# A two-layer diffusion block on one core: the context's hidden values loaded later and in pairs, its FFN output product begun from weight units still in the ring, and another order of the engines beside the first pair of FFN columns

## What is computed

```
for i in range(2):                      # layer 0: window attention || gated linear attention; layer 1: 2-D neighbourhood
    hl = rms_norm(xl, g) * (1 + sc1) + sh1      ;  hc = the same of the context xc
    yl, yc = mixer(hl, hc)
    xl = xl + gt1 * rms_norm(yl)
    xl = xl + gt2 * rms_norm(swiglu(rms_norm(xl) * (1 + sc2) + sh2))
    if i == 0:                          # the context is carried through layer 0 only
        xc = xc + cgt1 * rms_norm(yc)
        xc = xc + cgt2 * rms_norm(swiglu(rms_norm(xc) * (1 + csc2) + csh2))
swiglu(h) = (silu(g) * u) @ w_out,  [g, u] = h @ w_in,   2816 hidden columns
```

## Time and profile before

| | |
|---|---|
| time, median of 3 runs | 1626.89 us (1626.4 to 1628.17) |
| the profiled execution's own time | 1628.51 us |
| its span in the profile | 1626.7 us |
| PE busy | 1581.5 us, 97% of the span |
| DVE, ACT, POOL busy | 64%, 45%, 21% |
| granted clock, mean of the span | 0.995 |
| HBM | 187.97 MB read, 12.88 MB written |

### The profile page before, as it was taken

How to read it: one execution, slowest core, us unless ns; L and a number is a source line. 1 busy time by engine, 2 the same in 40 slices (tenths; PEclk the granted TensorE clock), 3 DMA queues, 4 the chain that set the end, 5 groups by cost and what they waited for, 6 DMA issues and landing times.

```text
span 1626.7 us, 27464 instructions
## 1 busy us (share of the span) xinstructions
PE 1581.5 (97%) x10334; PEld 1384.1 (85%) x10334; DVE 1042.4 (64%) x1710; ACT 738.1 (45%) x1401; POOL 333.7 (21%) x277
## 2 busy tenths in 40 slices
PE   6999999999899999998999999999999999999998
PEld 4878887778899999997887788888888899889986
DVE  5955567718988878867787533017872788258843
ACT  4342226737544444433336442237873645235632
POOL 2311233034000000000002044233433410420042
PEclk9999999999999999999999999999999999999999
DMA  9843211023154344337893539324012233323332
GB/s 356 276 130 82 50 27 53 2 78 91 50 169 128 114 141 142 121 139 247 320 321 131 168 114 243 86 78 130 16 53 77 73 97 109 125 80 106 108 113 76
DMA packets 176371, 204.21 MB, mean 126 GB/s; under 512 B 16664, under 2 KB 138864, under 8 KB 175856
## 3 DMA queue, kind: packets, MB, share of 16 engines
q1 hardware_dynamic: 162232, 156.62, 31.0%
q10 hardware_dynamic: 14008, 45.83, 8.7%
HBM read 187.97 MB, written 12.88 MB: 123 GB/s over the span
## 4 chain that ended last, share of the span: by engine, by line
PE 86%; DVE 5%; ACT 3%; issue 2%; DMA 1%; POOL 1%; SPq 0%; DVEq 0%; ACTq 0%; POOLq 0%
PE ps L2789 26%; PE ps L3347 18%; PE ps L2742 13%; PE ps L2966 11%; PE ps L3159 3%; PE ps L3102 3%; PE ps L3065 3%; PE ps L3022 2%; PE ps L2898 1%; PE ps L3043 1%; PE ps L2859 1%; PE ps L2771 1%; DMA mod_early<-in_w_mod 1%; DVE prob L2060 1%; ACT junk L1251 1%
## 5 line engine op out<-in xcount | busy, mean ns | idle before, releaser
L676 POOL TENSOR_TENSOR w_lo<-w_raw,w_hi 128x1024 fp32r<-128x1024 f32 (+2 forms) x88 | 219.9, 2501 | 642.2 <-ACT w_hi L1264 642.0
L1264 ACT ACTIVATE w_hi<-w_raw 128x1024 fp32r<-128x1024 f32 (+2 forms) x202 | 204.3, 1013 | 212.5 <-PE ps L2789 152.5
L676 DVE TENSOR_TENSOR w_lo<-w_raw,w_hi 128x1024 fp32r<-128x1024 f32 (+1 forms) x111 | 126.7, 1144 | 91.5 <-ACT w_hi L1264 91.3
L2742 PE MATMUL ps<-h_hi,w_hi 128*128 128x512 f32 (+1 forms) x480 | 142.8, 354 | 1.3 <-DVE h_lo L1866 1.1
L3347 PE MATMUL ps<-hc_hi,h_hi 128*128 128x384 f32 x420 | 141.0, 336 | 2.9 <-ACT x_u L1311 2.3
L3347 PE MATMUL ps<-hc_hi,h_lo 128*128 128x384 f32 x420 | 140.3, 334 | 0.0
L3347 PE MATMUL ps<-hc_lo,h_hi 128*128 128x384 f32 x420 | 140.3, 334 | 0.0
L2742 PE MATMUL ps<-h_hi,w_lo 128*128 128x512 f32 (+1 forms) x480 | 140.3, 349 | 0.0
L2742 PE MATMUL ps<-h_lo,w_hi 128*128 128x512 f32 (+1 forms) x480 | 139.5, 348 | 0.0
L2789 PE MATMUL ps<-w_hi,h_hi 128*128 128x512 f32 x408 | 128.1, 395 | 5.3 <-DVE w_lo L676 4.1
L2789 PE MATMUL ps<-w_lo,h_hi 128*128 128x512 f32 x408 | 126.7, 392 | 0.0
(11 more groups left out here) (404 smaller groups left out, 3864.4 us busy)
## 6 DMA issues: line engine op xcount, KB each, us to landing
w_raw<-in_w_ffn_in SPq DMA_DIRECT2D x88, 512.0 KB, 3.9
w_raw<-in_w_ffn_out SPq DMA_DIRECT2D x66, 512.0 KB, 3.9
mod_raw<-in_w_mod ACTq DMA_DIRECT2D x40, 512.0 KB, 6.1
mod_early<-in_w_mod SPq DMA_DIRECT2D x30, 512.0 KB, 10.1
w_raw<-in_na_w_in SPq DMA_DIRECT2D x29, 512.0 KB, 3.7
gate_b<-in_w_mod ACTq DMA_DIRECT2D x18, 512.0 KB, 4.6
hid_far<-full SPq DMA_DIRECT2D x22, 384.0 KB, 2.3
xs<-hid_far SPq DMA_DIRECT2D x22, 256.0 KB, 6.1
```

The lines of the kernel that those rows point to most:

```text
L676: eng.tensor_tensor(w_lo[:, ring(u), cols], w_raw[:, u % RAW, cols], w_hi[:, ring(u), cols].bitcast(F32), ALU.subtract).then_inc(low_ready ...
L1264: act.activation(w_hi[:, ring(u), cols], w_raw[:, u % RAW, cols], ACT.Copy).then_inc(w_hi_done, 1)
L2742: mm = pe.matmul(o[0], sta(x, o), mov(y, o), start=first and n == 0, stop=last and n == 2)
```

## The change

It does five things.

1. **`fo0C` keeps three units.** Its list of new units is cut from 22 to 19; the product begins with units 19, 20 and 21 of `fo0L`, which are in the ring, and takes k = 19, 20, 21 first. Its three early `feed`s among the norms become one (DVE) or none (ACT); PE waits once for all of `hidc_lo`.
2. **The context's hidden values later.** `hidc_turn(k)` says which context parts are handled in iteration k of `fo0L`: none for k under 5, then two in each of 5 to 9, then part k itself. All are split within `fo0L`.
3. **Another order beside pairs 0 and 1** on DVE and ACT: `combine_first` is cut into `first_half`, `first_sums` and `first_made`, which stand at three places; `part_copy(1)` and `part_sum(1)` stand ahead of the last split parts of `hc`; pair 1's jobs `s4` and `a22` are split earlier; sums and scales of the context's norm are interleaved otherwise.
4. **The last unit of `out0L`** gets its low part from DVE instead of POOL.
5. **A Silu of one column** (`warm`) right after the attention, so that ACT's table load stands there.

```diff
-    rows("fo0C", a["w_ffn_out"][0], range(FT))
+    rows("fo0C", a["w_ffn_out"][0], range(FT - KEPT))
...
+    by_dve[sp("out0L") + KT - 1] = True
...
-            for n, name in enumerate(("out0C", "v1C")):
+            for n, name in enumerate(("out0C", "fo0C", "v1C")):
                 if sp(name) <= u < sp(name) + KEPT:
                     eng.wait_ge(w_again, n * KEPT + u - sp(name) + 1)
...
+        def hidc_turn(k):
+            return (2 * k - 10, 2 * k - 9) if 5 <= k < 10 else (k,) if 10 <= k else ()
...
-                if sp("fo0L") + 3 <= u < sp("fo0C") + 3:
-                    hidc_load(u - sp("fo0L") - 3)
+                if sp("fo0L") + 6 <= u < sp("fo0C") + 1:
+                    for k in hidc_turn(u - sp("fo0L") - 1):
+                        hidc_load(k)
...
+            def part_copy(j):
+                act.wait_ge(s_used, NT + job(j, "s1") + 1)
+                act.wait_ge(f_11, NT + j)
+                act.activation(part_p, fast_ps(fast_banks(j)[2]), ACT.Copy).then_inc(fp_copied, 1)
...
                 for k in range(FT):
                     high_jobs(HID_JOB + k)
-                    if k >= 2:
-                        hidc_high(k - 2)
+                    for x in hidc_turn(k):
+                        hidc_high(x)
                     feed(sp("fo0L") + k)
...
             attention(0, 1, last_projection)
+            act.activation(warm[:], one_col[:], ACT.Silu)
...
             for p in range(PARTS):
                 hc_high(6, p)
             high_jobs(job(1, "s3"))
+            high_jobs(job(1, "a22"))
             for p in range(PARTS):
                 hc_high(3, p)
+            part_copy(1)
             for p in range(PARTS):
                 hc_high(5, p)
             high_jobs(job(1, "s2"))
-            act.wait_ge(fp_2, NT + 3)
-            act.activation(sum_11, fast_ps(fast_banks(0)[0]), ACT.Silu).then_inc(f_silu1, 1)
...
             attention(0, last_projection, rotate_add)
+            feed(sp("out0L") + KT - 1)
...
-            def combine_first():
+            def first_half():
...
+            hc_sum(1, 0)
+            hc_sum(2, 0)
             gated("out0C", 0, gb_need["out0C"])
...
             joined("out0C", 1, LT + 1)
-            hc_low(dve, 4, 0)
             pre_scale("ffn0C", 0, C_TILES)
...
             low_jobs(job(1, "s3"))
+            first_half()
             weight_sum(dve, 1, "s2")
             weight_sum(dve, 1, "s4")
             for p in range(PARTS):
                 hc_sum(4, p)
+            first_sums()
+            low_jobs(job(1, "s4"))
             for p in range(PARTS):
                 hc_low(dve, 3, p)
+            low_jobs(job(1, "a22"))
+            part_sum(1)
             for p in range(PARTS):
                 hc_low(dve, 5, p)
             low_jobs(job(1, "s2"))
...
-            tm_product("fo0C", FT, hidc_act, C_TILES, two_halves("fo0C"), before=claim_tile("fo0C"),
+            pe.wait_ge(hidc_lo_done, NT + FT)
+            tm_product("fo0C", FT - KEPT, hidc_act, C_TILES, two_halves("fo0C"), before=claim_tile("fo0C"), kept="fo0L",
                        after=lambda k: out_hooks[k]() if k in out_hooks else None)
```

More of the change, by code:

```diff
@@ L267, in build @@
     by_dve = [False] * n_units
-    for name, n, step in (("fo0L", FT, 1), ("fo0C", FT, 1), ("v1C", KT - KEPT, 1)):
+    for name, n, step in (("fo0L", FT, 1), ("fo0C", FT - KEPT, 1), ("v1C", KT - KEPT, 1)):
         for u in range(sp(name) + step - 1, sp(name) + n, step):
@@ L1308, in fast_in @@
                         break
[L1309 to L1312, removed]
+                    if j > 1:
+                        part_copy(j)
+                    if 1 < j < FT - 1:
                         high_jobs(job(j + 1, "s3"))
@@ L1693, in _ @@
             pre_square("ffn0C", 1, C_TILES, (post_x, POST["out0C"] + 2))
+            hc_high(4, 0)
             hc_high(2, 0)
[L1695 to L1698, removed]
+            pre_high("ffn0C", 0, C_TILES, whole=False)
+            act.wait_ge(fp_2, NT + 3)
+            act.activation(sum_11, fast_ps(fast_banks(0)[0]), ACT.Silu).then_inc(f_silu1, 1)
+            hc_high(4, 1)
+            hc_high(2, 1)
+            pre_high("ffn0C", 1, C_TILES, whole=False)
+            hc_high(4, 2)
+            hc_high(2, 2)
             for p in range(PARTS):
@@ L1731, in _ @@
             for k in range(FT):
-                feed(sp("fo0C") + k + RING)
+                feed(sp("fo0C") + k)
                 if k in hooks:
@@ L2468, in combine_first, with part_sum, sum_first @@
                 dve.tensor_tensor(second, second, columns3(sum_12[:]), ALU.mult).then_inc(hid_made, 1)
+            def part_sum(j):
+                dve.wait_ge(s_used, NT + job(j, "s3") + 1)
+                dve.wait_ge(fp_copied, NT + 2 * j + 1)
+                dve.wait_ge(f_22, NT + j)
+                dve.tensor_tensor(sum_t, fast_ps(fast_banks(j)[3]), part_p, ALU.add).then_inc(f_t, 1)
+            def sum_first(j):
+                dve.wait_ge(w_used, ring_no[sp("fi0") + 2 * j] + 1)
+                dve.wait_ge(fp_copied, NT + 2 * j + 2)
+                dve.tensor_tensor(sum_11, fast_ps(fast_banks(j)[0]), part_p, ALU.add).then_inc(f_11, 1)
             def gated(name, i, need):
@@ L2537, in _ @@
                     break
[L2538 removed]
+                if j == 1:
+                    sum_first(1)
                 if j + 1 < FT:
@@ L2548, in _ @@
                     weight_sum(dve, j + 1, "s4")
-                dve.wait_ge(w_used, ring_no[sp("fi0") + 2 * j] + 1)
-                dve.wait_ge(fp_copied, NT + 2 * j + 2)
-                dve.tensor_tensor(sum_11, fast_ps(a_), part_p, ALU.add).then_inc(f_11, 1)
+                if j > 1:
+                    sum_first(j)
                 low_jobs(job(j + 1, "s2") if j + 1 < FT else HID_JOB + 2)
@@ L2556, in _ @@
                 low_jobs(HID_JOB + k)
-                if k >= 2:
-                    hidc_low(k - 2)
+                for x in hidc_turn(k):
+                    hidc_low(x)
                 feed(sp("fo0L") + k)
                 add_rows(("fo0L", k))
-            for k in (FT - 2, FT - 1):
-                hidc_low(k)
             mix1 = range(NT)
             post_norm("fo0L", 0, 0, FT)
-            feed(sp("fo0C"))
             post_norm("fo0L", 1, 1, FT)
@@ L2568, in _ @@
             post_norm("fo0L", 2, 2, FT)
-            feed(sp("fo0C") + 1)
+            post_norm("fo0L", 3, 3, FT)
+            feed(sp("fo0C"))
             pre_scale("mix1", 1, mix1)
-            post_norm("fo0L", 3, 3, FT)
-            feed(sp("fo0C") + 2)
             hooks = {2: lambda: modulation(7), 3: lambda: (pre_modulate("mix1", 0, mix1), pre_scale("mix1", 2, mix1)),
@@ L2580, in _ @@
             for k in range(FT):
-                if k + RING < FT:
-                    feed(sp("fo0C") + k + RING)
+                if k < FT - KEPT:
+                    feed(sp("fo0C") + k)
                 if k in hooks:
@@ L2765, in again @@
                 def again(n, i, t, last):
-                    k = KT - KEPT + n
+                    k = (FT if kept == "fo0L" else KT) - KEPT + n
                     s = sp(kept) + k
```

52 lines of the change are left out of this document (26 added, 26 removed).

## The result

The changed kernel takes 1620.76 us, median of 20 executions, beside 1628.95 us for the kernel before: a ratio of 0.9949, 95% interval 0.9941 to 0.9958, or 8.2 us (6.8 to 9.6). The forecast was a ratio of 0.9942 and 1617.5 us. It is faster by more than the 0.2% that can be told from no change. But that the sum came out so near is in part luck: the gains are some 3 us larger than forecast, and the change costs 4 us or more in a way that the prediction does not name, by the addresses of tiles that TensorE reads. The two nearly cancel.

A forecast was written before the change was run, and what follows sets the result against it. PE bounds the kernel, working 1581.5 of 1626.7 us. Terms -0.9 - 2.5 - 3.5 - 2.5 = -9.4 us take the profiled 1628.51 to 1619.1, or 1617.5 from the median 1626.89; range 1612.0 to 1623.5.

The forecast's parts named there:

- What is at stake, 18.6 us: Eight PE waits where the change works, 14.1 us, plus lower clock behind two of them, 2.8 and 1.7 us.
- The last unit, -0.9: `out0L`'s tail: with the low part on DVE, PE's wait of 0.93 goes, -0.9 us.
- The first pairs, -2.5: Start of `fi0`: waits of 1.23, 2.31, 0.54 shrink or go, 2.53 for `hc` 4 stays, new 1.3 at pair 2.
- The start of `fo0L`, -3.5: The 4.07 wait at unit 2 and its 2.8 of clock go, 6.9 us; 3.5 kept after later limits.
- the second limit: `fo0L` soon after 786 us: DMA engines full, 1.9 us spare at unit 17, loads forward by only 1 to 2 us.
- The ring of pairs: `fo0L` iterations 5 to 9: two buffers, each pair loaded after the last is split; unit 10 ready at 795.3, 2.3 us lost.
- L = 5: Assumed time in us from issue to landing of a pair of context parts in `fo0L`.
- The start of `fo0C`, -2.5: With three units already in the ring, PE's waits of 1.12 and 1.40 for low parts go, -2.5 us.
- A: Rival: `fo0L` keeps its whole 6.9 us and pair 2's new wait doesn't come; 14.1 in all, 1612.8 us; chance 0.20.
- B: Rival: pairs land at 6.2 us, `fo0L` loses 1.4 instead of winning 3.5; 4.5 in all, 1622.4 us; chance 0.17.
- D: Rival: pairs land at 8.5 us, unit 10 of `fo0L` 12.9 later; 7.0 slower, 1633.9 us; chance 0.08.
- C: Rival: the first pairs give nothing, DVE's full list just moves the waits; 6.9 in all, 1620.0 us; chance 0.09.

The follow-up runs named there:

- x1_kept: The kernel before with only the three kept units of `fo0C` (with its feeds, norms and waits); 1626.25 us, 0.9982.
- x4_lastunit: The kernel before with only the low part of `out0L`'s last unit moved to DVE; 1627.97 us in one execution.
- y3_turn: The changed kernel with the context's second-tile turn ahead of pair 1's product 2 on PE, and `hc` 4's low parts ahead of `hc` 2's on DVE; 1619.87 us, 0.9954.
- z3_nowarm: The changed kernel without the warm Silu and without its tile; 1617.16 us, 0.9920.
- z1_wide: The changed kernel with the warm Silu's tile 16 columns wide instead of one, the Silu still writing one column; 1618.62 us, 0.9932.
- z4_best: The changed kernel with the 16-column warm tile, four buffers for the context's hidden values, and pair 2's low part made ahead; 1617.21 us, 0.9926.
- y1_nofirst: The changed kernel with the order beside pairs 0 and 1 as before, the other four edits kept; 1623.72 us, 0.9973.
- z2_pad: The kernel before with one more one-column tile behind `one_col` that nothing reads or writes, no instruction changed; 1634.26 us, 1.0033.
- y4_feed: The changed kernel with the low part of pair 2's first unit made right behind job `s3` on DVE; 1618.43 us, 0.9941.
- x3_first: The kernel before with only the other order beside pairs 0 and 1, the early Silu included; 1629.85 us, 1.0006.
- y2: The changed kernel with four buffers instead of two for the context's hidden values; 1619.62 us, 0.9946.

## Why the prediction was right, and where it was wrong

**What is at stake, 18.6 us.** The 1.7 us of clock behind the 2.53 were counted as loss of their own. They are not. In the trace before, product 3 of pair 1 starts 436.54 - 255.73 = 180.81 us after the first mark, with a clock of 0.83 and a wait of 2.31. In x1_kept the clock is 1.00 in that window, the wait is 3.93, and the start is 180.57 after the mark (a window, then PE's timeline):

```profile
420.00:430.00 10.00, 10.00 (x59) 10.00 (x59) 9.96 (x18) 4.76 (x9) 0.00 (x0) 1.00 0.17 50
```

```profile
436.49 0.69 PE L3341 MATMUL ps<-hc_hi,h_hi 128*128 128x384 f32 x1 [3.93 <-ACT x_u L1311]
```

A slower PE only waits less: ACT's and DVE's chain sets that moment. Behind it a lower clock does cost. In x1_kept and x4_lastunit the lower clock comes behind the wait of 3.93 instead, 0.76 and 0.71 over 430 to 440 us, and from product 3 of pair 1 to the first row of `fo0L` they take 303.5 and 303.7 us, where the kernel before takes 301.8: 1.7 and 1.9 more.

**The last unit, -0.9.** -1.2 in the stage (145.43 to 144.24): the 0.93, and 0.2 to 0.3 that no row explains. Right.

**The first pairs, -2.5.** Between the two traces `fi0` gives -1.7; over the traces without a star, 338.1 on average without the new order and 335.0 with it, -3.1. The -1.7 holds an estimated 0.8 of slow pace in the changed kernel's `fi0` (last section), without which it is the -2.5 of the forecast; the average is larger since three of its four traces without the new order have a lower clock behind product 3, as above. Each wait went as forecast: 1.23, 2.31 and 0.54 gone, 2.53 kept, and the new one for `w_lo` at 1.29 where 1.3 was said. Right, and for the reason given: DVE's full list, which y3_turn shows again. The table load of 1.28 did not have to leave for it: z3_nowarm, without the early Silu, waits no more than 0.40 at any product of pair 1. What the sum did not have is the slow pace.

**The start of `fo0L`, -3.5.** -4.4 between the two traces, -4.7 as the mean of seven traces with pairs and two buffers against five without pairs (121.6, 126.3), -6.1 from that mean of five to the best. The step that was mis-sized is the second limit, "all the spare there", the full DMA. The ring of pairs did what was worked out: from the first pair's issue to unit 10's low part 755 to 795.3, 40.3 us, was forecast, and the trace has

```profile
750.53 1.38 SPq L1042 DMA_DIRECT2D hidc_raw<-hid_far  x2
```

```profile
789.48 1.23 DVE L682 TENSOR_TENSOR w_lo<-w_raw,w_hi 128x1024 fp32r<-128x1024 f32 x1 [0.53 <-ACT w_hi L1271]
```

so 789.48 + 1.23 - 750.53 = 40.2. The ring itself can be seen: SP issues each pair right behind the split of the pair before, for instance

```profile
757.66 0.77 DVE L2446 TENSOR_TENSOR hidc_lo<-hidc_raw,hidc_hi 128x256 fp32r<-128x256 f32 x2 [0.94 <-ACT hidc_hi L1286]
```

```profile
758.11 0.80 SPq L1042 DMA_DIRECT2D hidc_raw<-hid_far  x2
```

and the five landings of the sum, those issued at 758.11, 763.54, 768.34, 775.85 and 782.18, took 3.5, 3.5, 6.6, 5.4 and 5.9 us, 5.0 in the mean, where L = 5 was a guess between the 3.6 and 10.5 measured. From unit 3's start at 750.57 to unit 10's at 790.85 are 2.2 us more than seven times 5.44, and 2.3 was said. But behind it nothing more is lost. The DMA engines are as full as before (1.04 at 409 GB/s in the window above, 1.02 at 379 in the earlier trace rows), and still unit 17's low part begins at

```profile
825.60 1.23 DVE L682 TENSOR_TENSOR w_lo<-w_raw,w_hi 128x1024 fp32r<-128x1024 f32 x1 [0.53 <-ACT w_hi L1271]
```

9.2 us sooner than at 834.78. Of these 4.5 lie ahead of `fo0L`, whose first row moved from 738.37 to 733.83; the other 4.6 fall within it, where the forecast allowed 1 to 2. I had taken a full DMA to move no sooner; the loads began earlier and kept their lead, at a rate that is 30 GB/s higher in these two windows. A wait of 1.27 in unit 18 of z3_nowarm and one of 0.79 in y3_turn, both behind the pairs, say that the full DMA does cost in some executions; I did not separate it further.

The landing of `hidc_raw` was 3.4 at least, 6.1 in the median, 8.4 at most (3.6, 6.2, 10.5 before). The estimated 2.3 us by the fit of the Trainium skill, page "DMA: Bandwidth & Descriptors", section "Anatomy of one DMA — SWDGE (gpsimd) path", is not in this trace either; that section is on transfers that GpSimd issues, and these are SyncE's.

**The start of `fo0C`, -2.5.** -1.9 between the traces. Without the address, in z3_nowarm, -3.1. Right in kind; that the gain needs the earlier end of the context parts, as x1_kept shows, was seen only as "costs nothing unless the ring of pairs lags".

**The term that is missing.** The fifth edit, `warm`, was read as an instruction. It also is a tile, and through the address of the tiles behind it it costs 1.2 in `fo0C`, 2.2 in the last stretch and, by an estimate from the matmuls' distances in the last section, 0.8 to 2.9 in `fi0` in the six traces that have it one column wide. At the quick pace the first pairs give -3.4 (338.1 to the 334.7 of z1_wide, z3_nowarm and z4_best). The sum is then -1.2 - 3.4 - 4.7 - 3.1 = -12.4 and 4.2 to 6.3 of cost, -8.2 to -6.1, beside 8.2 measured (6.8 to 9.6) and 9.4 forecast. Without the tile z3_nowarm measures 13.0 (10.6 to 15.3).

**The rivals.** A has some 6 of its 6.9 in `fo0L` in six of the nine traces with pairs (120.2 to 120.8), and its 1612.8 in none, since the new wait and the address are there. B and D are refuted: the five landings that count are 5.0 in the mean, though the median over all 22 parts is 6.1. (By the prediction's own line D decides from L = 7.1 on, not 7.0: 770.3 + 5 L = 805.8.) C is refuted by y1_nofirst and by `fi0`'s lengths.

## What to carry to other kernels

Read a diff for what it declares as well as for what it issues: a new small tile ahead of others moves their addresses, and a stage that is bound by TensorE can slow down far from the edit. Compare stage lengths over the whole span, not only the waits, since a slower pace shows in no wait. And before a wait is priced, ask whether the releasing engine has idle time behind it: where its list is full, clock and waits in front of it only trade places up to the moment which that list sets; a lower clock behind it costs time.

## What was not expected of the hardware

**The address of the stationary operand.** In `fo0C` and in layer 1's output product the moved tiles are the 128x128 operand that is held in TensorE while the other streams; matmuls there get 4 to 6 ns longer, in layer 1 from 390 to 395 or 396. Between the kernel before and z2_pad only the groups that read `hid`, `hidc` and `hc` get longer by more than 1 ns from `fi0` on (groups of over twenty matmuls). That the address and no other thing does it, z2_pad shows; that it is the stationary operand's is read from the groups that change. The Trainium skill, page "SBUF — State Buffer", section "Operand start alignment", asks only for a multiple of the element's size and says that its runs timed nothing. z2_pad shows that a legal address can cost 0.3% of a kernel (1.0033, 1.0020 to 1.0046).

**Two paces in `fi0` with the clock at 1.00.** In the five traces with a star PE does some 2% fewer matmuls over 100 us and more of `fi0`, without a wait. The same window in the changed kernel,

```profile
500.00:540.00 40.00, 40.00 (x232) 40.00 (x231) 33.77 (x52) 17.32 (x30) 0.00 (x0) 1.00 0.46 142
```

and in y4_feed:

```profile
500.00:540.00 40.00, 40.00 (x228) 40.00 (x227) 33.10 (x54) 17.92 (x32) 0.00 (x0) 1.00 0.42 130
```

The changed kernel has the slow pace too, for a shorter time. A later window in the kernel before, in the changed kernel and in z1_wide:

```profile
584.00:616.00 32.00, 32.00 (x187) 31.97 (x186) 25.37 (x42) 14.10 (x26) 0.00 (x0) 1.00 0.45 139
...
584.00:616.00 32.00, 32.00 (x184) 31.50 (x183) 26.63 (x43) 13.04 (x23) 0.00 (x0) 1.00 0.45 139
...
584.00:616.00 32.00, 32.00 (x187) 31.96 (x186) 27.00 (x44) 12.57 (x22) 0.00 (x0) 1.00 0.46 144
```

From one start of a matmul to the next the mean is 173.3 ns at one pace and 176.7 at the other. The slow one is in all seven traces whose moved tiles begin at 142496 (after, x3_first, y1, y2, y3, y4, z2_pad) and in none of the five at 142464 and the two at 142528, where no stretch of 20 us behind 460 us has a mean over 173.6. Here the moved `hc` tiles are the 384 columns that stream. So the slow pace goes with the shift of 32 bytes, in kernels with the change and without it (z2_pad). From the distances I estimate its cost at 0.8 us in the changed kernel and x3_first and 2.4 to 4.1 in the five with a star. No run was made for it, and what switches between the two paces within an execution is open.

**The lower clock is not the price of a wait.** The wait for `hc_lo` is 2.25 in z2_pad and 2.26 in x1_kept, with the same order of work, and the granted clock over 420 to 430 us is 0.83 in the first and 1.00 in the second. With the new order it is 0.83 over 410 to 420 in the changed kernel (wait 2.64) and 1.00 in x3_first (2.63).
